# Last down projection by seven block products in place of eight, activations standing

## What is computed

```python
def conv_ffn(h, w_up, conv_w, conv_b, w_down):
    u = h @ w_up                                   # 512x1024 @ 1024x5632
    s = u.shape[1]
    up = jnp.pad(u, ((0, 0), (CONV_WIDTH - 1, 0), (0, 0)))
    c = conv_b + conv_w[0] * up[:, 0:s]
    for j in range(1, CONV_WIDTH):
        c = c + conv_w[j] * up[:, j:j + s]
    val, gate = jnp.split(c, 2, axis=-1)
    return (jax.nn.silu(gate) * val) @ w_down      # 512x2816 @ 2816x1024
...
    h2 = rmsnorm(x, ffn_norm_g[l])
    x = x + conv_ffn(h2, w_up[l], conv_w[l], conv_b[l], w_down[l]).astype(x.dtype)
```

## Time and profile before

| | us |
|---|---|
| median of 3 runs | 1880.21 (1878.9 to 1881.28) |
| profiled execution, first to last instruction (its span) | 1881.8 |
| down projection, first to last product issued | 1753.49 to 1874.72 |
| TensorE busy, share of the span | 1818.0, 97% |
| GpSimd busy, share of the span | 1260.4, 67% |
| VectorE busy, share of the span | 777.2, 41% |
| ScalarE busy, share of the span | 440.5, 23% |

### The profile page before, as it was taken

The page is one execution under the profiler, slowest core; times in us unless marked ns, Lnnn a source line. Parts: engine busy times, 40 slices in busy tenths (PEclk is TensorE's granted clock), DMA queues, the critical chain, the costliest instruction groups (busy, mean ns, idle before and its releaser), DMA issues.

```text
span 1881.8 us, 29302 instructions
## 1 busy us (share of the span) xinstructions
PE 1818.0 (97%) x11443; PEld 1443.2 (77%) x11443; DVE 777.2 (41%) x1386; ACT 440.5 (23%) x893; POOL 1260.4 (67%) x621
## 2 busy tenths in 40 slices
PE   8999999999899999999999999998889999999998
PEld 6888888876577888888777875666767878888887
DVE  4333351057475333300445344415646255555201
ACT  3000001034531000000322255544424132212000
POOL 6888887855159888878585442332375868777773
PEclk9999999999999999999999999999999999999999
DMA  4232333222023322333342532140034323323331
GB/s 167 96 100 91 104 92 94 94 94 68 23 79 101 100 100 90 94 95 103 124 176 96 158 129 62 45 157 14 4 118 150 99 78 100 98 92 98 93 94 63
DMA packets 59787, 180.32 MB, mean 96 GB/s; under 512 B 7043, under 2 KB 13955, under 8 KB 58796
## 3 DMA queue, kind: packets, MB, share of 16 engines
q1 hardware_dynamic: 50140, 165.83, 27.4%
q10 hardware_dynamic: 9552, 13.13, 2.0%
HBM read 165.81 MB, written 13.13 MB: 95 GB/s over the span
## 4 chain that ended last, share of the span: by engine, by line
PE 91%; DVE 3%; ACT 2%; issue 2%; DMA 0%; SPq 0%; ACTq 0%; DVEq 0%
PE bank L562 25%; PE bank L563 25%; PE bank L564 25%; PE bank L978 1%; PE bank L1006 1%; PE bank L951 1%; PE bank L1167 1%; PE bank L659 1%; PE bank L580 1%; PE bank L581 1%; PE bank L584 1%; PE bank L913 1%; PE bank L1139 1%; PE bank L1152 0%; DMA x_tok<-x_dram 0%
## 5 line engine op out<-in xcount | busy, mean ns | idle before, releaser
L470 POOL TENSOR_TENSOR w_hi<-w_raw,one 128x1024 fp32r<-128x1024 f32 (+1 forms) x279 | 526.3, 1886 | 484.8 <-PE bank L564 419.3
L472 POOL TENSOR_TENSOR w_lo<-w_raw,w_hi 128x1024 fp32r<-128x1024 f32 (+1 forms) x279 | 683.2, 2449 | 21.9
L562 PE MATMUL bank<-h_hi,w_hi 128*128 128x512 f32 x1392 | 558.5, 401 | 5.2 <-DVE h_lo L1939 1.7
L564 PE MATMUL bank<-h_hi,w_lo 128*128 128x512 f32 x1392 | 543.4, 390 | 0.0
L563 PE MATMUL bank<-h_lo,w_hi 128*128 128x512 f32 x1392 | 543.3, 390 | 0.0
L562 PEld LDWEIGHTS bank<-h_hi,w_hi 128*128 128x128 f32 x1392 | 262.4, 189 | 70.8 <-issue 10.9
L563 PEld LDWEIGHTS bank<-h_lo,w_hi 128*128 128x128 f32 x1392 | 262.4, 189 | 60.5 <-issue 7.5
L564 PEld LDWEIGHTS bank<-h_hi,w_lo 128*128 128x128 f32 x1392 | 262.1, 188 | 55.0
L562 PE MATMUL bank<-a_hi,w_hi 128*128 128x512 f32 x528 | 205.5, 389 | 0.0
L564 PE MATMUL bank<-a_hi,w_lo 128*128 128x512 f32 x528 | 205.4, 389 | 0.0
L563 PE MATMUL bank<-a_lo,w_hi 128*128 128x512 f32 x528 | 205.4, 389 | 0.0
(11 more groups left out here) (387 smaller groups left out, 2183.6 us busy)
## 6 DMA issues: line engine op xcount, KB each, us to landing
w_raw<-w_ffn_gu_dram SPq DMA_DIRECT2D x88, 512.0 KB, 3.3
w_raw<-w_conv_up_dram SPq DMA_DIRECT2D x44, 512.0 KB, 3.5
w_raw<-w_ffn_down_dram SPq DMA_DIRECT2D x32, 448.0 KB, 3.3
w_raw<-w_ffn_down_dram SPq DMA_DIRECT2D x16, 512.0 KB, 3.5
w_raw<-w_out_dram SPq DMA_DIRECT2D x16, 512.0 KB, 3.5
w_raw<-w_gates_dram SPq DMA_DIRECT2D x16, 512.0 KB, 3.7
w_raw<-w_rwkv_dram SPq DMA_DIRECT2D x14, 512.0 KB, 3.5
w_raw<-w_conv_down_dram SPq DMA_DIRECT2D x16, 448.0 KB, 3.4
```

The lines of the kernel that those rows point to most:

```text
L470: nc.gpsimd.tensor_tensor(w_hi[:, s, 0:width], raw, one[:, 0:1].to_broadcast([P, width]), ALU.mult).then_inc(sem("w_rounded"), 1)
L472: nc.gpsimd.tensor_tensor(w_lo[:, s, 0:width], raw, w_hi[:, s, 0:width].bitcast(F32), ALU.subtract).then_inc(sem("w_split"), 1)
L562: nc.tensor.matmul(dst, hi, rhs_hi[:, k, :], start=start and k == k0, stop=False)
L564: last = nc.tensor.matmul(dst, lo, rhs_hi[:, k, :], start=False, stop=stop and k == k1 - 1)
```

## The change

The down projection is now one Strassen product (Winograd's form) in which the four blocks of a side are: token half by pairs of hidden tiles (even, odd) for the activations, and even/odd hidden tile by output half for the weights. It takes seven products of half blocks in place of eight. The activations are the standing operand (128 hidden by 128 tokens), and 512 output channels of a weight piece stream past. The result therefore has tokens on partitions and needs no transposing.

- It runs in 22 steps s. Steps 0 to 10 have four pieces each, steps 11 to 21 three: 77 pieces (`PIECES`) of six products, 462 in all. Seven sums over hidden tiles grow in banks 0 to 7, two banks (token tiles) to a group, three groups reusing their banks in steps 11 to 21. Between steps 10 and 11 VectorE and ScalarE combine the banks (`between_phases`).
- Weight sums: in steps 0 to 10 VectorE makes three 128x512 sums from two loaded tiles (`down_sums`), in steps 11 to 21 one.
- Activation sums: in the up projection, behind every second pair, VectorE makes four 128x256 sums from `a32`, which takes the place of `a_hi` and `a_lo`.
- Parts: ScalarE rounds each piece (`down_high`, 77 of 128x512) and each step's activation columns (`part_high`). GpSimd makes the low part of each piece (77 of 128x512, L662 now), and VectorE that of the activations (`part_low`: 128x256 and 128x768, then 128x512 and 128x256).
- x is transposed to token order during the up projection (`turn_x`, behind pair 1 and pair 9) and copied by ScalarE. VectorE adds it in (`with_x`).
- Loads: 22 tiles of 128x1024, and the second half of each odd tile once more (11 of 128x512).

The core of the diff:

```diff
+PIECES = [(s, i) for s in range(2) for i in range(4)]
+PIECES = [PIECES[i] for i in (0, 1, 2, 4, 5, 3, 6, 7)] + [(s, i) for s in range(2, JT) for i in range(4)]
+PIECES += [(s, i) for s in range(JT, 2 * JT) for i in range(3)]
...
+        def piece_free(q):
+            return nth("w_used", FIRST["conv_down"] + (q - 7 if q >= 8 else q // 2 - 3))
...
+            def load_b(s):
+                if s < 2:
+                    sp.wait_ge(*nth("w_split", down - RING + 2))
+                elif s < 5:
+                    sp.wait_ge(*nth("w_used", down))
+                else:
+                    sp.wait_ge(*nth("w_split", down + PLACE[s - 3, 3] + 1))
+                sp.dma_start(b_slot(s), w_conv_down[2 * s + 1, :, S:])\
+                    .then_inc(sem("w_in0") if s < 2 else sem(SHARED[f"b_in{(s - 2) % 3}"][0]), 16)
+            load_a(0)
+            load_b(0)
+            load_b(1)
+            load_a(1)
...
-            stream_down(FIRST["conv_down"])
+            for q in range(len(PIECES)):
+                pool.wait_ge(*nth("down_hi", q + 1))
+                nc.gpsimd.tensor_tensor(piece_place(w_lo, q), piece_source(q), piece_place(w_hi, q).bitcast(F32),
+                                        ALU.subtract).then_inc(sem("w_split"), 1)
...
+            for q, (s, i) in enumerate(PIECES):
+                pe.wait_ge(*nth("w_split", FIRST["conv_down"] + q + 1))
+                pe.wait_ge(*nth("a_part_ready", s + 1))
+                if s == 0 and i >= 2:
+                    pe.wait_ge(*nth("conv_a_ready", KF - 3 + i))
...
+                for t in range(2):
+                    nc.tensor.matmul(dst, part_hi[:, at], hi, start=begin, stop=False, skip_group_check=True)
+                    nc.tensor.matmul(dst, part_lo[:, at], hi, start=False, stop=False, skip_group_check=True)
+                    last = nc.tensor.matmul(dst, part_hi[:, at], lo, start=False, stop=end, skip_group_check=True)
...
+            def down_sums(s):
+                a = a_slot(s)
+                dve.wait_ge(*a_landed(s))
+                if s >= JT:
+                    j = s - JT
+                    dve.wait_ge(*nth("w_split", down + PLACE[j, 1] + 1))
+                    summed(nc.vector.tensor_tensor(sum2(j), sum2(j), a[:, 0:S], ALU.add))
+                    return
+                dve.wait_ge(*b_landed(s))
...
+                summed(nc.vector.tensor_tensor(b_slot(s), a[:, S:], b_slot(s), ALU.add))
+                summed(nc.vector.tensor_tensor(a[:, S:], a[:, 0:S], a[:, S:], ALU.add))
+                dve.wait_ge(*nth("down_sum", 3 * s + 1))
+                summed(nc.vector.tensor_tensor(sum2(s), b_slot(s), a[:, 0:S], ALU.add))
...
+            with dve.Fori(0, JT - 2) as i:
                 conv_pair(i)
+            down_sums(0)
+            conv_pair(JT - 2)
+            down_sums(1)
+            part_low(0)
+            conv_pair(JT - 1, lambda: part_low(1))
+            down_sums(2)
...
+            for s in range(2, 2 * JT):
+                if s + 1 < 2 * JT:
+                    down_sums(s + 1)
+                part_low(s)
+                if s == JT:
+                    between_phases()
+                elif JT + 3 <= s < JT + 6:
+                    with_x(s - JT - 3)
```

More of the change, by code:

```diff
@@ new lines, in conv_silu, with conv_pairs, copy_x @@
+            def conv_silu(i, u):
+                act.wait_ge(*nth("conv_taps", 2 * (2 * i + u) + 2))
+                nc.scalar.activation(bank[2 * u + 1][:, :], tmp[:, 1, :], ACT.Silu).then_inc(sem("conv_silu"), 1)
+            def conv_pairs(first, end):
+                with act.Fori(first, end) as i:
+                    for u in range(2):
+                        for v in range(2):
+                            conv_tap(i, u, v)
+                        conv_silu(i, u)
+            def copy_x(half):
+                act.wait_ge(*nth("conv_h_ready", KD))
+                for n in range(NT):
+                    act.wait_ge(*nth("out_turned", NT * half + n + 1))
+                    nc.scalar.activation(x_tokens(n, half), by_channel(bank[4 + n][:, :]), ACT.Copy)\
+                        .then_inc(sem("out_copied"), 1)
@@ new lines, in part_high @@
+            def part_high(s):
+                act.wait_ge(*nth("a_sums", s + 1 if s < JT else JT))
+                if s:
+                    act.wait_ge(*part_free(s))
+                for at, source in part_sources(s):
+                    nc.scalar.activation(a_parts[s % 2][0][:, at, :], source, ACT.Copy)\
+                        .then_inc(sem(SHARED["a_part_hi"][0]), 1)
+            conv_pairs(0, 1)
+            copy_x(0)
+            conv_pairs(1, 5)
+            copy_x(1)
+            conv_pairs(5, JT - 1)
@@ new lines, in part_low @@
+            def part_low(s):
+                dve.wait_ge(*nth("a_sums", s + 1 if s < JT else JT))
+                for x, (at, source) in enumerate(part_sources(s)):
+                    dve.wait_ge(*nth("a_part_hi", 2 * s + x + 1))
+                    hi, lo = (part[:, at, :] for part in a_parts[s % 2])
+                    last = nc.vector.tensor_tensor(lo, source, hi.bitcast(F32), ALU.subtract)
+                last.then_inc(sem(SHARED["a_part_ready"][0]), 1)
+            with dve.Fori(0, JT - 2) as i:
+                conv_pair(i)
@@ new lines, in with_x @@
+            def with_x(which):
+                dve.wait_ge(*nth("out_copied", KD))
+                for t in range(2):
+                    if which == 0:
+                        nc.vector.tensor_tensor(by_channel(a32[:, t, :]), by_channel(kept(C22, t)), x_tokens(2 + t, 1),
+                                                ALU.add).then_inc(sem("end_x_ready"), 1)
+                    elif which == 1:
+                        stepped(nc.vector.tensor_tensor(by_channel(kept(W_SUM, t)), by_channel(kept(V_SUM, t)),
+                                                        x_tokens(t, 1), ALU.add))
+                    else:
+                        stepped(nc.vector.tensor_tensor(by_channel(kept(Q1_COPY, t)), x_tokens(2 + t, 0),
+                                                        by_channel(kept(V_SUM, t)), ALU.subtract))
@@ L2695, in _layouts @@
         w_merge=merge, w_out_2=blocks(one["w_out_2"]), w_conv_up=pairs(one["w_up_2"]),
[L2696 removed]
+        w_conv_down=one["w_down_2"].reshape(KF, P, D))
 def kernel(**inputs):
```

259 lines of the change are left out of this document (200 added, 59 removed).

## The result

The changed kernel takes 1912.6 us (median of 4 runs, 1906.7 to 1916.5) against 1880.3 (1878.9 to 1881.3): ratio 1.0161, 95% interval 1.0145 to 1.0177. So it is slower, by 32 us between the medians and by 30 us by that ratio. The forecast was 1911. Its profiled execution has a span of 1914.7.

A forecast was written before the change was run, and what follows sets the result against it. The prediction took the down projection to be bound by TensorE's products, with VectorE and GpSimd taking turns after the change. Terms -15.0 - 1.1 + 10.0 + 1.6 + 35.6 = +31.1 gave span 1912.9, median 1911 us, range 1890 to 1928.

The forecast's parts named there:

- Parts 1 and 2: Down projection: 528 products become 462, -15.0 us; transposes moved to the up projection and a shorter tail, together -1.1 us.
- Part 3: Before pair 20: TensorE stalls because VectorE's step 0 sums wait for loads, +10.0 us; lower clock afterwards, +1.6 us.
- Part 4: Entry into the down projection: VectorE late, TensorE stands until part_low(1) at 9.3 us; part_low(2) at 22.5.
- Part 5: Steps 2 to 10: five VectorE and four GpSimd instructions in turn, 7.3 us a step against TensorE's 5.44.
- Parts 6 and 7: Bank combining, part_low(12) at 91.2 us; steps 12 to 21 at 4.7 each; last product at 140.3. Parts 4 to 7: +35.6.
- the floor of exclusive time, 128.7: Down projection: GpSimd and VectorE work that can't overlap, 128.7 us in all, so at least +24 us.
- VectorE's sums 1.7, GpSimd's low parts 1.6: Sign in the profile after: VectorE's 512-column sums average near 1.7 us, GpSimd's low parts near 1.6.
- About 10 us once ahead of pair 20: Sign: TensorE waits about 10 us once ahead of pair 20 for VectorE's product of pair 18.
- Part_low ends TensorE's waits: Sign: in steps 2 to 10 part_low ends TensorE's idle time, every 7.3 us.
- The clock did fall: Rival, down projection steps: TensorE's clock stays at the lower level and sets the pace, 1930 to 1965 us; chance 0.08.
- the two engines don't hold each other up: Rival: VectorE and GpSimd run undisturbed; only the pair 20 stall and some 6 us of entry remain, 1882 us; chance 0.08.
- The third, 1864: Rival: VectorE's wait for slot 0 doesn't reach TensorE and no lock holds, leaving -16.1, 1864 us; chance 0.04.

The follow-up runs named there:

- GpSimd short: The changed kernel with GpSimd computing only 8 of 512 columns of each weight low part in the last down projection: 1880.2 us.
- waits filled: Against low parts on VectorE: sums and low parts put into VectorE's waits for ScalarE, step 1 rounded earlier, last pair's activation sums later: 1871.2 us.
- sums later: The changed kernel with VectorE's weight sums of step 0 moved behind pair 19 instead of ahead of pair 18: 1906.6 us.
- low parts on VectorE: Against sums later: VectorE instead of GpSimd computes the weights' low parts in the last down projection, some placed in its waits: 1873.8 us.
- VectorE short: The changed kernel with most of VectorE's sums and activation low parts in the last down projection cut to 8 columns, GpSimd whole: 1881.2 us.

## Why the prediction was right, and where its parts were not

- **Parts 1 and 2** (products -15.0, transposes and tail -1.1). The counts are right, and the second sum too. The price of a product was taken from the old kernel and is a little low for the new ones: where TensorE doesn't wait they start 0.2303 apart on average and not 0.2267 (GpSimd short), which makes 461 of them 1.6 us longer. In the changed kernel the turns hide that; where TensorE sets the pace, it counts. The up projection grew by 234.6 - 231.1 = 3.5 us in a run without the stop (waits filled against before); the tail is 1914.7 - 1910.6 = 4.1, 4.0 predicted.
- **Part 3** (stop +10.0, low clock +1.6). The place, the cause and the sum are right: up to the end of the up projection the changed kernel lost 246.2 - 231.1 - 3.5 = 11.6, the sum of the two terms (though 8 x 0.19 is 1.5 and not 1.6). The terms were shifted: some 8.6 of standing and 3.0 of slow products. The two halves of pair 18 took VectorE 3.1 and 4.6 us (1737.99 to 1741.10 to 1745.73), not 3.4 and 4.9. That the sums end at 1738.07 is the forecast's 1732.6 plus the 5.4 by which this profile lies later there (1.9 in the first tap, 3.5 of transposes).
- **Part 4** (entry). This step failed in size. Step 2 was to start at +22.5 and started at 1788.1 - 1770.5 = +17.6. Four halves of pairs at 0.3 us too much each, and sums of step 1 of which only two met GpSimd, put the end of pair 20 at +1 where it was -2.9. So part_low(1) ended at +4.5 and not +9.3, and the stall ahead of it was 0.27 and not 5.2. Also GpSimd stood idle from 1779.2 to 1782.6, waiting for ScalarE, so that five of the six sums there took 0.69 and not a turn each. The one long stall left was 5.9, ahead of step 2.
- **Part 5** (7.3 us a step). The mechanism is right, the count of turns was not. I counted four of GpSimd's a step, since TensorE uses four. As long as GpSimd has room ahead it takes one turn for each of VectorE's, five a step: VectorE's part_low of steps 2 to 5 start at 1784.55, 1792.96, 1801.47 and 1809.90, 8.4 apart (5 x 1.11 + 2.75 = 8.3). Later it has to wait for free places, and steps of 6.3 and 7.4 follow. From part_low(2) to part_low(10) it is 57.8 us (1842.36 - 1784.55), in place of 56.1.
- **Parts 6 and 7.** TensorE had part_low(12) at 1859.4, +88.9, predicted 91.2: of the 4.9 us that the entry came out shorter, 2.3 are left. From part_low(12) to part_low(21) it is 1902.58 - 1856.10 = 46.5, predicted 42.4 + 3.3 = 45.7. The last product started at 1910.37, 139.9 behind the first, predicted 140.3. The terms of the prediction as written, 91.2 + 42.4 + 3.3 + 4.1, give 141.0 for its end, so 140.8 for its start; the half us between is the weight sum that the last of the nine intervals lacks, which it leaves unsaid. And part_low(21) wasn't what set the end: TensorE's last wait, at 1902.22, is for part_low(20). So an entry that was put 4.9 too long was made up by steps that were put too short: that the sum is right to 0.4 us is in part luck. That it is near is not, because of the floor of exclusive time, 128.7, under the whole.
- **Signs.** "VectorE's sums 1.7, GpSimd's low parts 1.6": 1.53 to 1.66 and 1.57 to 1.67. "About 10 us once ahead of pair 20": 8.6. "Part_low ends TensorE's waits": 14 times of 14. Two signs were missed: of the waits of 5 and 6 us in the entry only the second came (0.27 and 5.9), and the steps came every 8.4 us at first and 6.3 to 8.5 us later, not every 7.3.
- **Rivals.** The clock did fall (1780 to 1790: 0.79; 1790 to 1800: 0.87) but TensorE had time to spare in the steps, with VectorE busy for 10.00 of 10 us in both windows, so it cost little there; no run held the clock up to show that. That the two engines don't hold each other up is refuted by both short runs; with VectorE's instructions at their own length the time was indeed the 1882 that this rival gave (1880.2). The third, 1864, needs no lock and no stop: the run with filled waits shows it to be a fair floor, 348.4 against 343.3 for the stage, 1.6 of the difference being the slower pace of the products.

## What to carry to other kernels

By these runs: before work is spread over VectorE and GpSimd, add up the time of both for whatever reads SBUF with two inputs on VectorE and at all on GpSimd: it is one budget, not two. Here nine instructions a step on VectorE alone took 28.6 us less of stage than five there and four on GpSimd (352.1 against 380.7, sums later in both, a few low parts put into waits in the one). A fill on GpSimd, or an input in PSUM on VectorE, is outside that budget. And an instruction that waits for a load belongs behind those that TensorE waits for: one line moved was worth 9.7 us.

## What the runs showed that was not expected

- A copy on GpSimd (one input) holds VectorE up until it ends, exactly like a difference: VectorE ends 0.54 behind it. A fill of the same columns doesn't.
- The engine that is ahead takes as many turns as the one behind, so five and not four a step while its buffers have room.
- A stop of TensorE of 3.5 us was followed by 5 us at granted clock 0.50, a loss of 2.6 (low parts on VectorE). One of 8.57 was followed by a loss of 3.0 in one profile of the changed kernel and 2.5 in the other, one of 2.08 by 1.7 (VectorE short). So a short stop can cost nearly as much behind it as a long one, and nearly twice its own length.
- Some 2.1 to 2.7 us of the down projection are in no wait of the profile, in every variant that TensorE bounds. The starts of its products show what they are. 1.6 is a slower pace: in even steps the products start 0.2331 apart on average and in odd ones 0.2267 to 0.2287, though both have the same sizes (GpSimd short: steps 6, 7 and 8 start at 1803.96, 1809.55 and 1815.00, so 5.59 and 5.45). The rest stands directly behind each wait, in the two products that follow it. Even and odd steps use different buffers (`a_parts[s % 2]`); whether that is why stays open.
- Identical code ahead of the stage ended anywhere between 1518.0 and 1524.3 us in eleven profiles. A single execution can be off by 3 us from that alone, which is as much as some of the differences asked for; the medians of the kernel before lie within 1.4 (1880.2 to 1881.6). The length of the stage in the two profiles of the changed kernel repeated to 0.2 (390.43 and 390.25).
